# A two-layer hybrid transformer on one core: memory keys of layer 2 moved to the front, modulation by quarters, the norm of x as a diagonal factor, a ring of nine slots

## The reference

```python
def first_block(x, c, w_ada, b_ada, g_mix, w_in, ...):
    c_act = jax.nn.silu(c)
    mod = c_act @ w_ada[l] + b_ada[l]
    sh1, sc1, gt1, sh2, sc2, gt2 = jnp.split(mod[:, None, :], 6, axis=-1)
    h = rmsnorm(x, g_mix[l]) * (1.0 + sc1) + sh1
    x = x + gt1 * hybrid_mixer(h, w_in[l], ...)
    h = rmsnorm(x, g_ffn[l]) * (1.0 + sc2) + sh2
    x = x + gt2 * conv_glu_ffn(h, ...)
    return rmsnorm(x, final_g)
...
    mkv = mem @ w_mem_kv
    m_k, m_v = mkv[..., :W], mkv[..., W:]
    y_m = memory_attention(head_rms_norm(heads(m_q), qk_g[2]), head_rms_norm(heads(m_k), qk_g[3]), heads(m_v))
```

## Time and profile before

| | us |
|---|---|
| median of 3 runs | 3166.49 |
| lowest, highest | 3163.52, 3172.57 |
| span of the profiled execution, first to last instruction | 3165.1 |
| PE busy in it | 3109.9 (98%) |
| DVE busy | 1983.7 (63%) |
| ACT busy | 1481.3 (47%) |
| HBM read | 654.41 MB, 207 GB/s over the span |

### The profile page before, as it was taken

The page is one execution under the profiler, slowest core; times in us unless marked ns, Lnnn a source line. Parts: engine busy times, 40 slices in busy tenths (PEclk is TensorE's granted clock), DMA queues, the critical chain, the costliest instruction groups (busy, mean ns, idle before and its releaser), DMA issues.

```text
span 3165.1 us, 38821 instructions
## 1 busy us (share of the span) xinstructions
PE 3109.9 (98%) x14412; PEld 2584.6 (82%) x14412; DVE 1983.7 (63%) x2082; ACT 1481.3 (47%) x1740; POOL 106.8 (3%) x206
## 2 busy tenths in 40 slices
PE   7899999999999999999999999999999999999999
PEld 6777878788888888888888888888888888888887
DVE  4878777876566566766555565646575565565564
ACT  2345445445444444555445435544445444444543
POOL 1211110100000000000000000000000000000000
PEclk7889999999999999999999999999999999999999
DMA  8888787775555555555555545555555555546555
GB/s 327 330 318 326 287 306 258 283 276 179 192 188 189 188 184 188 171 173 178 183 177 190 191 151 187 180 189 181 176 173 169 194 171 195 176 159 196 168 184 191
DMA packets 179989, 658.45 MB, mean 208 GB/s; under 512 B 20080, under 2 KB 20368, under 8 KB 179216
## 3 DMA queue, kind: packets, MB, share of 16 engines
q1 hardware_dynamic: 150992, 550.51, 51.9%
q0 software_dynamic: 28864, 106.08, 9.0%
HBM read 654.41 MB, written 2.10 MB: 207 GB/s over the span
## 4 chain that ended last, share of the span: by engine, by line
PE 95%; DVE 2%; DMA 1%; issue 1%; ACT 0%; SPq 0%; POOL 0%; DVEq 0%; ACTq 0%
PE pg L1019 29%; PE pg L1021 29%; PE pg L1020 29%; PE pm L1054 1%; PE pm L1073 1%; PE pm L1515 1%; DVE R L1636 1%; DMA w_raw<-w 1%; PE pm L1102 1%; DMA R<-w_ada 0%; PE pm L1409 0%; DVE w_lo L1720 0%; PE pm L1145 0%; PE pm L1086 0%; PE pm L1144 0%
## 5 line engine op out<-in xcount | busy, mean ns | idle before, releaser
L1564 DVE TENSOR_TENSOR w_lo<-w_raw,w_hi 128x1024 fp32r<-128x1024 f32 x888 | 1085.7, 1224 | 974.1 <-ACT w_hi L496 969.4
L496 ACT ACTIVATE w_hi<-w_raw 128x1024 fp32r<-128x1024 f32 x888 | 941.0, 1060 | 1336.8 <-PE pg L1021 1316.6
L1019 PE MATMUL pg<-w_hi,hT_hi 128*128 128x512 f32 x3232 | 1289.5, 399 | 45.0 <-DVE w_lo L1720 34.5
L1021 PE MATMUL pg<-w_hi,hT_lo 128*128 128x512 f32 x3232 | 1272.8, 394 | 0.0
L1020 PE MATMUL pg<-w_lo,hT_hi 128*128 128x512 f32 x3232 | 1272.6, 394 | 0.0
L1019 PEld LDWEIGHTS pg<-w_hi,hT_hi 128*128 128x128 f32 x3232 | 616.4, 191 | 175.9 <-issue 39.3
L1021 PEld LDWEIGHTS pg<-w_hi,hT_lo 128*128 128x128 f32 x3232 | 615.3, 190 | 130.9
L1020 PEld LDWEIGHTS pg<-w_lo,hT_hi 128*128 128x128 f32 x3232 | 616.8, 191 | 125.4 <-issue 0.5
L1019 PE MATMUL pg<-w_hi,y_parts 128*128 128x512 f32 x864 | 338.0, 391 | 1.4 <-issue 1.4
L1021 PE MATMUL pg<-w_hi,y_parts 128*128 128x512 f32 x864 | 336.4, 389 | 0.0
L1020 PE MATMUL pg<-w_lo,y_parts 128*128 128x512 f32 x864 | 336.2, 389 | 0.0
(11 more groups left out here) (275 smaller groups left out, 1364.8 us busy)
## 6 DMA issues: line engine op xcount, KB each, us to landing
w_raw<-w SPq DMA_DIRECT2D x1028, 512.0 KB, 3.5
R<-w_ada POOLq DMA_DIRECT2D x196, 512.0 KB, 6.2
R<-mem_T SPq DMA_DIRECT2D x4, 512.0 KB, 9.9
x_rows<-x SPq DMA_DIRECT2D x1, 2048.0 KB, 21.1
R<-mem_T SPq DMA_DIRECT2D x1, 2048.0 KB, 11.0
out<-x_rows SPq DMA_DIRECT2D x4, 512.0 KB, 5.1
con_sb<-con SPq DMA_DIRECT2D x1, 1344.0 KB, 9.1
small_w_sb<-small_w POOLq DMA_DIRECT2D x2, 576.0 KB, 4.5
```

The source lines that it names most:

```text
L496: act.activation(w_hi[:, g % RING, :, :].rearrange("p c n -> p (c n)"), raw[:, g % RING, :], ACT.Copy).then_inc(hi_done, 1)
L1019: pe.matmul(out, hi, w_hi[:, slot, c, :], start=start, stop=False)
L1021: return pe.matmul(out, lo, w_hi[:, slot, c, :], start=False, stop=stop)
L1564: tt(flat(w_lo[:, g % RING, :, :]), raw[:, g % RING, :], flat(w_hi[:, g % RING, :, :]).bitcast(F32), ALU.subtract).then_inc(lo_done, 1)
```

## The change

The keys of layer 2 (mk1) now follow mv0 as tiles 16 to 23; x and y come in four pieces of two tiles each (24 to 39), one piece per quarter of the modulation; all from p to o3 is eight tiles later, and mv1 (128 to 135) ends the front, which still has 136 tiles. Scale and shift are made in quarters, each from 16 chunks of which DVE takes 12 and PE four (k = 1, 5, 9, 13), and PE adds DVE's accumulator into the same PSUM columns. The first 64 chunks go through nine slots, the later ones through five. The rows of x are no longer scaled: PE multiplies them by a diagonal matrix of the row factors. Root and reciprocal of the head norms are split from the squares. SP's order is changed, and so is where the constants `con1` live.

```diff
-FRONT = ("mk0", "mv0", "x", "y", "p", "q0", "k0", "v0", "q1", "k1", "v1", "o0", "o1", "o2", "o3", "mk1", "mv1")
+FRONT = ("mk0", "mv0", "mk1", "x", "y", "p", "q0", "k0", "v0", "q1", "k1", "v1", "o0", "o1", "o2", "o3", "mv1")
-F_TILES += [(u, j) for first in (0, GT // 2) for u in (F_X, F_Y) for j in range(first, first + GT // 2)]
+F_TILES += [(u, j) for r in range(QUARTERS) for u in (F_X, F_Y) for j in (2 * r, 2 * r + 1)]
+ADA_SLOTS = (14, 15, 16, 17, 18, 4, 5, 6, 7)
+HALVES = [((1, 4 * r, 4), (0, 4 * r, 4)) for r in range(QUARTERS)]
+HALVES += [((q, 8 * e, 8),) for q, e in ((4, 0), (3, 0), (2, 0), (2, 1), (4, 1), (3, 1), (5, 0), (5, 1))]
+def of_pe(h, k):
+    return h < QUARTERS and k % 4 == 1
...
-        xn_1 = slot(4, TB, D)
+        diag = slot(1, TB, P)
-        con1 = mk_T[:, 1, :, :].rearrange("p h s -> p (h s)")
+        con1 = con[:, 2 * P:2 * P + NCON1]
...
         def _(sp):
-            sp.dma_start(vec[:, :], t["vec"]).then_inc(vec_in, 16)
-            sp.dma_start(con[:, 0:2 * P], t["con"][:, 0:2 * P]).then_inc(con_in, 16)
-            for p in range(4):
-                sp.dma_start(mem_f[:, 4 * p:4 * p + 4, :], t["mem_T"][:, 4 * p:4 * p + 4, :]).then_inc(mem_in[p], 16)
...
+                else:
+                    sp.dma_start(mem_f[:, 4 * g:4 * g + 4, :], t["mem_T"][:, 4 * g:4 * g + 4, :]
+                                 ).then_inc(mem_in[g], 16)
                 tile(g, g)
-                if g == 3:
+                if g == 0:
+                    sp.dma_start(vec[:, :], t["vec"]).then_inc(vec_in, 16)
+                    sp.dma_start(con[:, 0:2 * P], t["con"][:, 0:2 * P]).then_inc(con_in, 16)
+                if g == 6:
                     sp.dma_start(x[:, :, :], t["x"]).then_inc(x_in, 16)
-                if g == 5:
+                if g == 26:
...
-                if g == 30:
-                    sp.dma_start(con[:, 2 * P:], t["con"][:, 2 * P:]).then_inc(late_in, 16)
-                if g == 104:
+                if g == 112:
                     sp.wait_ge(y_ready, 2)
                     sp.dma_start(mem_f1, t["mem_T"]).then_inc(mem1_in, 16)
+                    sp.dma_start(con[:, 2 * P:], t["con"][:, 2 * P:]).then_inc(late_in, 16)
...
         def _(pool):
+            pool.wait_ge(mem_in[0], 16)
...
 -                p = g - RING - 128
-                if 0 <= p < GT:
-                    act.wait_ge(hf_done, GT + p + 1)
+                for p in range(2 * (g - FT), 2 * (g - FT) + 2):
+                    if 0 <= p < GT:
+                        act.wait_ge(hf_done, GT + p + 1)
...
         def _(pe):
+            def rows_T_normed(q):
+                for c in range(KC):
+                    k = q * KC + c
+                    for tb in range(TB):
+                        i = pe.matmul(pm[q % 3][:, c * S + tb * P:c * S + (tb + 1) * P], x[:, tb, k * P:(k + 1) * P],
+                                      diag[:, tb, :], start=True, stop=True)
+                i.then_inc(rowsT_ps, 1)
+            mod_bias(0)
+            for n, at in enumerate((4, 7, 10)):
+                upto(at)
+                mod_chunk(0, 4 * n + 1)
+            upto(12)
+            pe.wait_ge(rows_ready, 1)
...
+            for r, steps in ((1, (17, 18, 20, 22, 23)), (2, (24, 25, 26, 27, 27)), (3, (28, 29, 30, 31, 31))):
+                upto(steps[0])
+                if r >= 2:
+                    pe.wait_ge(mod_taken, r - 1)
+                mod_bias(r)
+                for n in range(4):
+                    upto(steps[n])
+                    mod_chunk(r, 4 * n + 1)
+                upto(steps[4])
+                mod_rest(r)
...
 -            weighs.update({i: [(0, 2 * i), (0, 2 * i + 1)] for i in range(8)})
-            weighs.update({8 + i: [(2, 2 * i), (2, 2 * i + 1)] for i in range(8)})
-            weighs.update({17 + i: [(3, k) for k in range(16 * i // 6, 16 * (i + 1) // 6)] for i in range(6)})
+            for n, c in enumerate(early):
+                at = 2 + n if n < 12 else 14 + (n - 12) * 10 // 12 if n < 24 else 24 + (n - 24) // 3
+                weighs.setdefault(at, []).append(c)
-                i = ts(xn_1[:, tb, :], x[:, tb, :], rstd[:, tb:tb + 1], None, ALU.mult)
+                i = ts(diag[:, tb, :], ident, rstd[:, tb:tb + 1], None, ALU.mult)
...
+            for r in range(QUARTERS):
+                if r == 3:
+                    upto(32)
+                    mem_squares(1)
+                upto(17 if r == 0 else 21 + 4 * r)
+                take_quarter(r)
+                modulated(r)
+                upto(22 + 4 * r)
+                lower_4(P_MIX + r, hf_1)
+            mem_normed(1)
...
-            upto(FT)
-            mem_heads(1)
             upto(FT + RING)
+            dve.wait_ge(hT_ready, P_FF + GT)
             step(dve.memset(flat(F_acc), 0.0))
```

More of the change, by code:

```diff
@@ L63 @@
 G_LAYER = G_FF + 3 * NFF
[L65 to L71, removed]
+HALVES = [((1, 4 * r, 4), (0, 4 * r, 4)) for r in range(QUARTERS)]
+HALVES += [((q, 8 * e, 8),) for q, e in ((4, 0), (3, 0), (2, 0), (2, 1), (4, 1), (3, 1), (5, 0), (5, 1))]
+CHUNKS = [(h, k) for h in range(len(HALVES)) for k in range(-1 if HALVES[h][0][0] in (2, 5) else 0, KD)]
+def of_pe(h, k):
+    return h < QUARTERS and k % 4 == 1
+ADA_PLACE, ADA_TURN, ADA_BEFORE = [], [], []
+for _i, (_h, _k) in enumerate(CHUNKS):
+    _ring = len(ADA_SLOTS) if _h < QUARTERS else ADA_RING
+    _first = 0 if _h < QUARTERS else QUARTERS * KD
+    ADA_PLACE.append((_i - _first) % _ring)
+    _used = [_n for _n in range(_i) if ADA_PLACE[_n] == ADA_PLACE[_i]]
+    ADA_TURN.append(len(_used) + 1)
+    ADA_BEFORE.append(_used[-1] if _used else None)
 IN2 = 15
@@ L275, in build @@
         ada_acc = [slot(13, AH), slot(12, AH)]
-        ada_ring = slot(14, ADA_RING, AH)
+        ada_at = [slot(i, AH) for i in ADA_SLOTS]
         Zx, Zy, Zp = slot(0, TB, NW), slot(2, TB, NW), slot(8, TB, NW)
@@ L406, in chunks_used @@
         def chunks_used(h):
-            return sum(1 for i, _ in CHUNKS if i <= h and i not in PE_HALVES)
+            return sum(1 for i, k in CHUNKS if i <= h and not of_pe(i, k))
         def chunks_before(i, by_pe):
-            return sum(1 for h, _ in CHUNKS[:i] if (h in PE_HALVES) == by_pe)
-        def turn(h):
-            return DVE_HALVES.index(h)
+            return sum(1 for h, k in CHUNKS[:i] if of_pe(h, k) == by_pe)
         P_MEM0, P_MIX, P_Y, P_MEM1, P_FF = 0, 4, 8, 16, 24
@@ L466, in _ @@
         def _(pool):
+            pool.wait_ge(mem_in[0], 16)
             for i, (h, k) in enumerate(CHUNKS):
[L468 to L472, removed]
+                before = ADA_BEFORE[i]
+                if before is not None:
+                    by_pe = of_pe(*CHUNKS[before])
+                    pool.wait_ge(ada_pe if by_pe else ada_used, chunks_before(before + 1, by_pe))
+                pool.dma_start(ada_at[ADA_PLACE[i]], t["w_ada"][i]).then_inc(ada_in[ADA_PLACE[i]], 16)
+                if i == chunk_at(4, 10):
                     pool.wait_ge(zf_ps, 1)
@@ L1109, in broadcast @@
                 for n in range(2):
-                    i = pe.matmul(pm[bank + n][:, :], ones, ada_acc[turn(h) % 2][:, n * NW:(n + 1) * NW], start=True,
+                    i = pe.matmul(pm[bank + n][:, :], ones, ada_acc[h % 2][:, n * NW:(n + 1) * NW], start=True,
                                   stop=True)
@@ L1214, in _ @@
             for gate in range(2):
-                upto(39 + 3 * gate)
+                upto(47 + 3 * gate)
                 pe.wait_ge(lru_act, 2 + 2 * gate)
@@ L1672, in _ @@
             fed = 0
-            weighs = {16 + 8 + i: [(4 + i // KD, i % KD)] for i in range(6 * KD)}
-            weighs.update({i: [(0, 2 * i), (0, 2 * i + 1)] for i in range(8)})
-            weighs.update({8 + i: [(2, 2 * i), (2, 2 * i + 1)] for i in range(8)})
-            weighs.update({17 + i: [(3, k) for k in range(16 * i // 6, 16 * (i + 1) // 6)] for i in range(6)})
+            weighs = {32 + i: [(4 + i // KD, i % KD)] for i in range(6 * KD)}
+            early = [c for c in CHUNKS if c[0] < QUARTERS and not of_pe(*c)]
+            for n, c in enumerate(early):
+                at = 2 + n if n < 12 else 14 + (n - 12) * 10 // 12 if n < 24 else 24 + (n - 24) // 3
+                weighs.setdefault(at, []).append(c)
             outs_at = {F_END[F_OUT + n] - 1 + RING: n for n in range(NB)}
@@ L2405 @@
     out1 = column_tiles(a["w_out"][0][order])
-    stream = [memory[0]]
+    stream = [memory[0], memory[1][:GT]]
     columns = [column_tiles(w1[:, c:c + NW]) for c in starts]
@@ L2414 @@
     bias[0] = a["b_ada"][0]
-    ada = [(bias if k < 0 else ada[k])[:, HALVES[h][0] * D + HALVES[h][1] * AH:][:, :AH] for h, k in CHUNKS]
+    blocks = [[q * KD + first + i for q, first, n in half for i in range(n)] for half in HALVES]
+    ada = [np.concatenate([(bias if k < 0 else ada[k])[:, b * P:(b + 1) * P] for b in blocks[h]], axis=1)
+           for h, k in CHUNKS]
     def ff(name, j):
```

349 lines of the change are left out of this document (168 added, 181 removed).

## The result

The changed kernel takes 3140.66 us (median of 4 runs, 3136.8 to 3144.15), the kernel before 3167.22 (median of 4, 3163.52 to 3172.57): a ratio of 0.9904, with a 95% interval of 0.9885 to 0.9924. The spans of the profiled executions are 3135.0 and 3165.1, a gain of 30.1.

What follows compares the result with a forecast made beforehand. PE was busy 98% of the span, but DMA bytes were taken to set the pace up to tile 32. From the span of 3165.1: -29.0 + 4.5 - 3.5 = -28, 3137.1; plus 1.4 for the median, given as 3138, range 3120 to 3157.

Steps and rivals of the forecast that it cites:

- The first 32 tiles: Work up to tile 32, compared with the old start of tile 24: gain 29.0 us, bounds 11 and 42.
- T: Start time of tile 32 in the changed kernel: forecast 168 us, from 61 MB at 370 GB/s, bounds 155 to 186.
- tile 24 at 113: Sign to look for in the changed kernel: tile 24 starts near 113 us.
- DMA is the highest floor: Up to tile 32: DMA's floor 155 to 186 us, above PE's 142 and DVE's 133, so queue filling sets T.
- PE is the chain: Rival, chance 0.14: small matmuls and DVE waits keep PE at 1.2 GHz in tiles 24 to 31; T = 180, total 3150.
- Late constants: At tile 112: 1344 KB of constants behind the memory, ahead of tile 113, cost 4.5 us, between 3.5 and 5.9.
- the old stall of 2.43: At tile 112, before the change: PE waits 2.43 us for the residual; forecast to become 6 to 8.
- The end of the front: From tile 136: 7.5 us saved by the vanished wait, 4 given back at tile 140; net 3.5 saved, bounds 0 and 7.5.
- The wait at tile 140: PE waits about 2 us for tile 140's low part, plus 2 for a slow tile: 4 given back.
- The start: First memory part and tile 0 lead the SP queue: PE starts at about 10 instead of 21; 11 us not booked separately.
- The diagonal factor: Transposes of x's rows become matmuls, 7.0 instead of 3.2 us on PE: +3.8, hidden as long as bytes set T.

Runs made afterwards that it cites:

- half_bytes: Changed kernel, fetching only half of the columns of the first 64 modulation chunks, that half read twice so the work keeps its size; 3126.82 us, 0.9866 to before.
- light_pe: Changed kernel with one small matmul in place of eight in each of PE's 16 modulation chunks, same bytes; 3132.47 us, 0.9884 to before.
- late_mem: Changed kernel with the second memory load moved from tile 112 to 116 and the constants to tile 131; 3128.68 us, 0.9874 to before.
- old_start: Changed kernel with the old order of the first transfers: vectors, constants and all memory ahead of tile 0, POOL's chunks at once; 3146.7 us, 0.9908 to before.
- five_transposed: Changed kernel with five chunk slots, and x's rows scaled on DVE and transposed on PE instead of multiplied by the diagonal matrix; 3144.84 us, 0.992 to before.
- all3: Changed kernel with the edits of late_mem and memset_split together; 3122.3 us, 0.9837 to before.
- spread: Changed kernel with the chunks of the last three quarters dealt evenly over tiles 15 to 32, PE's moved with them; 3138.11 us, 0.9893 to before.
- five_slots: Changed kernel with five slots in the chunk ring instead of nine; 3151.94 us, 0.995 to before.
- half_light: Changed kernel with the edits of half_bytes and light_pe together; one run, 3123.17 us.
- memset_split: Changed kernel with the accumulator cleared in two halves, at tiles 136 and 138, not ahead of tile 140's low part; 3133.54 us, 0.9884 to before.

## Why the prediction was right

The forecast was 3138 (3120 to 3157), the result 3140.66. Against the span it was -28, measured -30.1. By its own steps:

- **The first 32 tiles: -29.0, measured -29.4.** T = 168 was right to 0.4 us, and tile 24 at 113 to 0.6 (113.56). The mean flow to T, 371 GB/s by the three windows, is the 370 of the prediction. But the reason was too simple. "DMA is the highest floor, so T is set by how well the queues stay full" is borne out by half_bytes for tiles 24 to 32 (9.5 us less with fewer bytes) and in part for 0 to 12 (3.4 us less, with the DMA engines full at 412 GB/s). Between them PE is the bound, which half_bytes and light_pe show, and 370 is a mean of 412, 326 and 378 that no single stretch has. The prediction compared its floors over all 32 tiles at once, where DMA is the highest. Its own prices would have shown the change of bound: 12 tiles at 2.72, six chunks at 1.9, two sums at 1.7, a set of transposes at 0.8 and the normed rows at 7.0, most of which fall here, are up to 55 us of PE work for tiles 12 to 24, which took 53.1. That the middle between two rates met the mean of three stages to 0.4 us is luck.
- **The rival "PE is the chain"** had its place in tiles 24 to 31, where the chunk and the sums were to leave PE at 1.2 GHz with T = 180. PE is the chain in tiles 12 to 24 instead, and at full clock (1.00). In 24 to 32 the clock is indeed low, 0.78, but light_pe, with seven eighths of the chunks' work on PE gone, did not shorten this stretch, so PE was not what set it.
- **Late constants: +4.5, measured +5.4.** The mechanism was as written: the wait of PE is 7.84 us (6 to 8 expected), for the residual behind a late tile. The price lay near the upper of the two given, 5.9 by the memory's own pace in that place, not near the 3.5 by 397 GB/s. The 4.5 was a value chosen between them. late_mem shows that this term and the old stall of 2.43 with it were avoidable.
- **The end of the front: -3.5, measured -8.3.** This is the term that was mis-sized, beyond its bound of 7.5. The wait at tile 136 is gone with its slow tile (5.45 and 2.0), as forecast. The wait at tile 140 is 2.54 for the 2 of the forecast, but no slow tile followed: tile 140 took 2.81, so 4 lost became 2.6. That was the luck of this trace. The same wait, 2.53 to 2.55, stands in eight kernels made from after; in seven of them tile 140 took 4.2 to 4.3 us, which makes the 4 of the forecast, and in one 2.85. With such a tile the end of the front would have come to 6.9, inside the bound. And the wait ahead of the FFN's last rows, which I had left unchanged, fell from 1.95 to 1.00 with no slow tile after it (it was 4.4). Together 2.7. In before it is the start of tile 124, in after that of tile 132 (529.54 above):

  ```profile
  530.36 0.77 PE L1019 MATMUL pg<-w_hi,hT_hi 128*128 128x512 f32 x1 [1.95 <-DVE w_lo L1720]
  ```

  The key transposes of layer 2, 0.8, had moved from tile 144 to tile 34 and came back here.
- **Not in the sum: +2.5 between tiles 32 and 111.** 0.8 is those transposes; the rest, 1.7, is the clock in code that did not change, and less than the same code varies by (see the last section).
- **The start** was seen at 10.35 where about 10 was written, but "they only lift a floor" undersold it: 5.6 us of T hang on it (old_start). They are inside T, so the sum did not suffer.
- **The diagonal factor: "hidden as long as the bytes set T".** Since they don't in tiles 12 to 24, up to 3.6 us of it (five_transposed) may be on the path; with nine slots this was not measured.

Not tried: chunks for PE in slots of their own, so that POOL doesn't stand behind PE. That its waits of up to 18.02 us keep the flow at 326 GB/s is a reading of the trace, and what it would bring is open; half_bytes, with 9.5 us from tile 24 to 32, shows about what more bytes at hand can bring there. Nor does any run price the quarters and the new order of the chunks by themselves: taken singly, the four slots (14.6) and the start (5.6) are 20 of the front's 29.4 us.

## What to carry to other kernels

Split a stage that has several near-equal floors at the places where the mix changes, and ask in each piece which engine is busy for all of it: a mean rate can be right while the bound changes twice within it. A large transfer put in a queue of tiles costs where the tile behind it is on someone's path (5.4 us here), and two such transfers in places of their own cost nothing in late_mem; this move and the split clearing together brought 11.4 us on the path in all3, against 30.1 for the whole change. And judge an edit by the starts of the tiles around it first, since the span also holds the clock's changes elsewhere. Even a tile right behind a wait can be a matter of one execution, as tile 140 shows.

## What the runs showed of the hardware

**Bytes.** One core moved 412 GB/s over 49 us, for the most part with transfers of 512 KB on two queues. The Trainium skill (DMA: Bandwidth & Descriptors, "Where 436 GB/s comes from") has HBM bind such transfers at about 358 GB/s; the trace does not agree.

**The clock in unchanged code.** The stretch from tile 32 to tile 111 is the same work in after and in nearly all kernels made from it (spread has a sum more in it). It took 285.5 us in five_slots, 290.4 in after and 296.5 in half_light: 11 us apart, with a mean granted clock of 0.98, 0.96 and 0.94, and PE never waited in it. Tile by tile nearly all of the difference sits in three places: at tiles 37 and 38 (the forget-gate product, 64 records of small matmuls), 68 and 69, and 92 and 93. In each of the latter two stand 16 records each of two kinds of small matmuls; taken together between 170 and 460 us they show what differs, first in five_slots, then in half_light (busy time, and mean ns of one):

```profile
L1178 PE MATMUL pm<-mv,con_sb 8*128 8x256 f32 x32 | 11.6, 443 | 0.0
L1177 PE MATMUL pm<-R 128*128 128x256 f32 x32 | 11.2, 433 | 0.0
```

```profile
L1179 PE MATMUL pm<-mv,con_sb 8*128 8x256 f32 x32 | 14.8, 551 | 0.0
L1178 PE MATMUL pm<-R 128*128 128x256 f32 x32 | 14.0, 526 | 0.0
```

The same 32 records of L1178 (L1179 in half_light, whose lines stand one lower) take a mean of 443 ns in one trace and 551 in the other, with no wait ahead of them (idle 0.0). The clock falls to 1.2 GHz while such small matmuls run, without any idle time of PE before, and the tile behind them is slow too. The forget-gate product of after shows it, in PE's timeline and in two windows, over the product and behind it:

```profile
185.05 10.54 PE L1240 MATMUL pm<-small_w_sb,R 128*128 128x8 f32 x64
```

```profile
185.10:196.00 10.90, 10.90 (x66) 10.82 (x65) 0.27 (x2) 0.00 (x0) 0.11 (x1) 0.65 0.09 35
196.00:197.30 1.30, 1.30 (x5) 0.99 (x4) 1.27 (x3) 0.96 (x2) 0.94 (x2) 0.50 0.12 25
```

At which of the small matmuls it falls differs from trace to trace though the code there is the same. What decides it stays open, and so does whether it goes with the kernel or with the execution: there is one trace per kernel, and the times of one kernel spread too, five_slots' over 13 us (3147.67 to 3160.77). Its size, 11 us between the ends, is about that of a whole experiment here. Of the 2.4 us of memset_split that the edit does not explain, 1.7 lie in this stretch; of light_pe's 9.1, 4.8 do.

**One-column matmuls at either clock.** A sum or a chunk of 16 records (eight matmuls in two passes) takes about half as long at the upper clock. In after the chunk at 130.75 ran at a granted clock of 1.00, the sum at 158.89 at 0.50:

```profile
130.75 1.84 PE L1127 MATMUL pm<-sc,R 128*128 128x1 f32 x16
158.89 3.58 PE L1135 MATMUL pm<-con_sb,R 128*128 128x1 f32 x16 [1.98 <-DVE R L1679]
```

The prediction priced every sum at 1.7 us, the value at the upper clock.
